# Low halves of the gate weight slabs: from GpSimd's subtraction to an accumulating DMA

## What is computed

```
def conv_glu_ffn(h_norm, w_in, conv_w, conv_b, w_out):
    gate, up = jnp.split(h_norm @ w_in, 2, axis=-1)      # w_in: 1024 x 5632
    padded = jnp.pad(gate, ((0, 0), (CONV_WIDTH - 1, 0), (0, 0)))
    conv = conv_b
    for t in range(CONV_WIDTH):                          # 3 taps over the tokens
        conv = conv + padded[:, t:t + S, :] * conv_w[t]
    return (jax.nn.silu(conv) * up) @ w_out              # w_out: 2816 x 1024
```

## Time and profile before

| | us |
|---|---|
| median of 3 runs | 1417.29 |
| lowest and highest run | 1416.80, 1419.93 |
| span of the profiled execution, first to last instruction | 1418.1 |

### The profile page before, as it was taken

The page is one execution under the profiler, slowest core; times in us unless marked ns, Lnnn a source line. Parts: engine busy times, 40 slices in busy tenths (PEclk is TensorE's granted clock), DMA queues, the critical chain, the costliest instruction groups (busy, mean ns, idle before and its releaser), DMA issues.

```text
span 1418.1 us, 17472 instructions
## 1 busy us (share of the span) xinstructions
PE 1400.8 (99%) x6863; PEld 1149.9 (81%) x6863; DVE 766.2 (54%) x1120; ACT 621.9 (44%) x1080; POOL 666.8 (47%) x371
## 2 busy tenths in 40 slices
PE   8999999999999999999999999999999999999999
PEld 6888778887788888888888887788778888888887
DVE  5574675565776305663165655836657652066611
ACT  6747482755433212333346555735753322132321
POOL 5635654552444444444346367535344444444443
PEclk9999999999999999999999999999999999999999
DMA  6332002331233323333333220223223333333322
GB/s 181 94 97 72 18 23 88 115 106 58 76 117 90 102 91 104 104 89 97 97 90 102 86 60 15 75 68 112 89 67 97 104 89 97 100 97 97 100 91 87
DMA packets 176305, 125.67 MB, mean 89 GB/s; under 512 B 14657, under 2 KB 152672, under 8 KB 176224
## 3 DMA queue, kind: packets, MB, share of 16 engines
q1 hardware_dynamic: 175664, 124.55, 29.5%
q10 hardware_dynamic: 560, 0.01, 0.0%
HBM read 122.44 MB, written 2.10 MB: 88 GB/s over the span
## 4 chain that ended last, share of the span: by engine, by line
PE 95%; DVE 2%; issue 1%; ACT 1%; DMA 1%; SPq 0%; DVEq 0%
PE bank L639 28%; PE bank L643 28%; PE bank L641 28%; PE bank L813 2%; PE bank L942 1%; PE bank L943 1%; PE bank L801 1%; PE bank L1022 1%; PE bank L982 1%; DVE Q L1831 1%; PE bank L1097 1%; DVE scores_h L1863 1%; PE bank L921 1%; DMA x_tok<-in_x 1%; DVE scores_g L1863 1%
## 5 line engine op out<-in xcount | busy, mean ns | idle before, releaser
L565 POOL TENSOR_TENSOR w_lo<-raw,w_hi 128x1024 fp32r<-128x1024 f32 (+2 forms) x230 | 545.9, 2377 | 664.8 <-ACT w_hi L1173 663.2
L1173 ACT ACTIVATE w_hi<-raw 128x1024 fp32r<-128x1024 f32 (+3 forms) x229 | 236.5, 1035 | 331.0 <-PE bank L643 330.6
L639 PE MATMUL bank<-x_hi,w_hi 128*128 128x512 f32 x944 | 371.4, 393 | 3.3 <-issue 1.6
L643 PE MATMUL bank<-x_hi,w_lo 128*128 128x512 f32 x944 | 367.5, 389 | 0.0
L641 PE MATMUL bank<-x_lo,w_hi 128*128 128x512 f32 x944 | 367.4, 389 | 0.0
L639 PEld LDWEIGHTS bank<-x_hi,w_hi 128*128 128x128 f32 x944 | 177.2, 188 | 46.1 <-issue 6.5
L641 PEld LDWEIGHTS bank<-x_lo,w_hi 128*128 128x128 f32 x944 | 177.2, 188 | 37.4 <-issue 1.4
L643 PEld LDWEIGHTS bank<-x_hi,w_lo 128*128 128x128 f32 x944 | 177.2, 188 | 37.3
L1950 DVE SCALAR_TENSOR_TENSOR conv<-gate_in,gains_all,conv 128x512 f32<-128x512 f32 x44 | 118.1, 2685 | 1.6
L1537 ACT ACTIVATE conv_silu<-conv 128x512 f32<-128x512 f32 x44 | 27.8, 632 | 169.5 <-DVE conv L1951 169.5
L1673 DVE TENSOR_TENSOR h<-h,bank 128x512 f32<-128x512 f32 x48 | 31.8, 681 | 105.2 <-PE bank L643 105.1
(11 more groups left out here) (318 smaller groups left out, 2276.2 us busy)
## 6 DMA issues: line engine op xcount, KB each, us to landing
raw<-in_w_ffn_in SPq DMA_DIRECT2D x88, 512.0 KB, 3.8
raw<-in_w_ffn_out SPq DMA_DIRECT2D x40, 512.0 KB, 3.6
raw<-in_w_in SPq DMA_DIRECT2D x27, 512.0 KB, 3.8
raw<-in_w_mix_out SPq DMA_DIRECT2D x16, 512.0 KB, 3.9
raw<-in_w_ca_kv SPq DMA_DIRECT2D x32, 256.0 KB, 3.2
raw<-in_w_ca_q SPq DMA_DIRECT2D x8, 512.0 KB, 3.4
raw<-in_w_ca_out SPq DMA_DIRECT2D x8, 512.0 KB, 3.8
raw<-in_w_in SPq DMA_DIRECT2D x12, 256.0 KB, 2.9
```

The source lines that it names most:

```text
L565: pool.tensor_tensor(w_lo[gi % SPLIT][:, c0:n], raw[gi % RAW][:, c0:n], w_hi[gi % SPLIT][:, c0:n].bitcast(f32), ALU.subtract).then_inc(S[" ...
L639: pe.matmul(o, ah, bh, start=first, stop=False)
L643: mm = pe.matmul(o, al, bh, start=False, stop=last)
L1173: act_.activation(w_hi[k % SPLIT][:, 0:n], raw[k % RAW][:, 0:n], ACT.Copy).then_inc(S["hi_split"], 1)
```

## The change

For the gate slabs alone, the low half is made otherwise. ACT writes `w_lo = -raw`, rounded to fp32r, which is the negated high half, ahead of its copy to `w_hi` (semaphore `negated`). POOL, in place of its subtraction, waits for `negated` and issues a DMA that adds `raw` to `w_lo` (`accum_op=ALU.add`), whose landing counts 16 on `lo_in` of the buffer. PE and SP wait for that semaphore, and for `hi_split` besides. All other slabs keep POOL's subtraction.

```diff
+    FIRST_DMA_LOW = slab_at["gate", 0, 0]
+    slab_names = {i: name for name, i in slab_at.items()}
+    pool_lows, dma_lows = {}, {}
+    for gi in range(DEPTH * NS):
+        if gi % NS >= FIRST_DMA_LOW and slab_names[gi % NS][0] == "gate":
+            dma_lows[gi] = 16 * (sum(j % SPLIT == gi % SPLIT for j in dma_lows) + 1)
+        else:
+            pool_lows[gi] = len(pool_lows) + 1
...
+        def low_ready(gi):
+            return (lo_in[gi % SPLIT], dma_lows[gi]) if gi in dma_lows else (S["lo_split"], pool_lows[gi])
...
                         if gi >= RAW:
-                            sp.wait_ge(S["lo_split"], gi - RAW + 1)
+                            sp.wait_ge(*low_ready(gi - RAW))
+                            if gi - RAW in dma_lows:
+                                sp.wait_ge(S["hi_split"], gi - RAW + 1)
...
+                        if gi in dma_lows:
+                            pool.wait_ge(S["negated"], sum(j <= gi for j in dma_lows))
+                            pool.dma_start(w_lo[gi % SPLIT][:, 0:n], raw[gi % RAW][:, 0:n], accum_op=ALU.add).then_inc(lo_in[gi % SPLIT], 16)
+                            continue
                         pool.wait_ge(S["hi_split"], gi + 1)
...
-                        pe.wait_ge(S["lo_split"], i + 1)
+                        pe.wait_ge(*low_ready(i))
+                        if i in dma_lows:
+                            pe.wait_ge(S["hi_split"], i + 1)
...
                             if k >= SPLIT:
                                 act_.wait_ge(*released[k - SPLIT])
+                            if k in dma_lows:
+                                act_.activation(w_lo[k % SPLIT][:, 0:n], raw[k % RAW][:, 0:n], ACT.Copy, scale=-1.0).then_inc(S["negated"], 1)
                             act_.activation(w_hi[k % SPLIT][:, 0:n], raw[k % RAW][:, 0:n], ACT.Copy).then_inc(S["hi_split"], 1)
```

More of the change, by code:

```diff
@@ L306, in build_trunk @@
         pb = [ctx.enter_context(nc.psum_tensor(f"bank{i}", [P, 512], f32)) for i in range(8)]
-        names = """lo_split hi_split slab_used spread_in mem_in rows_t gains_ready chain_v chain_a chain_p
+        names = """lo_split hi_split negated slab_used spread_in mem_in rows_t gains_ready chain_v chain_a chain_p
             hT_mm h_in h_sq_done h_sq_sum r_cols_mm hk_mm hk_evac x_hi_done x_lo_done r_done r_diag_done r_mm r_bc_done
@@ L320, in build_trunk @@
         raw_in = [ctx.enter_context(nc.semaphore(f"raw_in{i}")) for i in range(RAW)]
+        lo_in = [ctx.enter_context(nc.semaphore(f"lo_in{i}")) for i in range(SPLIT)]
+        def low_ready(gi):
+            return (lo_in[gi % SPLIT], dma_lows[gi]) if gi in dma_lows else (S["lo_split"], pool_lows[gi])
         x_in = [ctx.enter_context(nc.semaphore(f"x_in{t}")) for t in range(NT)]
@@ L391, in build_trunk @@
         PER_LAYER = dict(
-            lo_split=NS, hi_split=NS, spread_in=16 * (1 + len(spread_of)), mem_in=16 * MT, zeroed=7, pair_prod=1, lat_sq_sum=2, tab_done=8,
+            spread_in=16 * (1 + len(spread_of)), mem_in=16 * MT, zeroed=7, pair_prod=1, lat_sq_sum=2, tab_done=8,
             qk_prod=1, scores_base=2 * NT, decays_done=len(BLOCKS), k_level=2 * len(BLOCKS), h_sq_done=3 * KD, h_sq_sum=3, r_cols_mm=2, rope_mm=1, lat_mm=4,
```

## The result

The changed kernel takes 1425.87 us (median of 4 runs, 1423.85 to 1429.09) against 1417.33 us before; the ratio is 1.0063, with an interval of 1.0051 to 1.0075. That is 8.5 us or 0.6% slower. The profiled execution has a span of 1422.1 us, at the fast end of its runs, and only 4.0 us over that of before. That difference of two executions is not the cost: before's execution lost some 4.1 us at 138 to 197 us, where the changed kernel's did not, far from anything the change touches; the changed kernel's lost 1.6 us at 840 us.

The account below looks back on a forecast made before the run. PE was taken to bound the kernel. With D = 5.7, waits of 2.36 and 3.15 us in layer 0, 2.36 and 2.71 in layer 1 made 10.6 us, added to the 1417.29 median: 1427.9 us, range 1419.5 to 1442.3.

Parts of the forecast that it names:

- What bounds the kernel: PE, busy 1400.8 of 1418.1 us at the 2.4 GHz level; only its waits matter, relieving POOL is worth nothing.
- The four tight places: gate(0,1) and gate(0,3) in both layers: 2.55 to 3.34 us until PE's first use; waits there sum to 10.6 us.
- gate(0,4) is covered by the wait at gate(0,3): Layer 0: gate(0,4) has only 4.15 us, but PE's wait at gate(0,3) delays its use and not its split.
- D: Time from the negation's end through POOL's issue, DMA and semaphore until PE may start; taken as 5.7 us.
- POOL and DVE: DVE's taps and POOL's subtractions hold each other up; first tap 0.55 us alone, 2.32 beside gate(0,3)'s subtraction.
- Relief of some 2 to 4 us reaches DVE only from chunk 2 on. Worth nothing on PE's path.: Fewer POOL subtractions free DVE only where gate slabs have enough slack; no gain for PE.
- I cost the negations at nothing: 44 negations of 1.05 us on ACT, 46 us, taken as hidden; uncovered at the four tight places, 4 us.
- PE waits D - S: At a gate slab PE waits D less S, the time from the old split's end to PE's first use.
- Rival A: The DMA lands like a plain load, D under 3.75 us, so it is hidden and the time not slower; chance 0.13.
- Rival B: Slow accumulation, D over 6.85 us: gate(1,0), then every second rhythm slab waits; 1444 us at 8; chance 0.25.
- Rival C: DVE's relief reaches PE through chunks 0 and 1, at most 1.3 us; 0.02 with anything else gaining over 0.2%.

Follow-up runs that it names:

- spare_tight: Changed kernel with gate(0,1) and gate(0,3) of both layers back on GpSimd's subtraction, 40 DMAs kept: 1417.61 us, ratio to before 1.0002.
- up_later: Accumulating DMA for 38 up slabs, all but up(0,0), up(0,1), up(0,3) of each layer, instead of the gate slabs: 1415.81 us, ratio to before 0.9987.
- tight_only: Changed kernel with the DMA only for gate(0,1) and gate(0,3) of both layers, the other 40 gate slabs subtracted: 1429.46 us, ratio to before 1.0081.
- negate_only: Changed kernel without accumulating DMAs: ACT negates all 44 gate slabs, then POOL subtracts over them as before: 1421.29 us, ratio to before 1.0023.
- late_1: Changed kernel with one idle memset on POOL ahead of each accumulating DMA: 1437.13 us, ratio to before 1.0136.
- late_2: Changed kernel with two idle memsets on POOL ahead of each accumulating DMA: 1470.03 us, ratio to before 1.0370.
- after_again: The changed kernel once more, word for word, with its own profile: 1425.61 us, ratio to before 1.0059.
- up_slabs: Accumulating DMA for 42 up slabs, all but up(0,0), instead of the gate slabs: 1417.19 us, ratio to before 0.9997.

## Why the prediction was right, and what was off in it

The forecast was 1427.9 us, +10.6; measured were +8.5, inside the range, by the mechanism that was named. That it came as close as it did is partly luck: a term that was too large and one that was missing made up for each other. By its steps:

- **What bounds the kernel.** Right in the main: forty of the 44 exchanges left the time as it was (spare_tight). POOL's busy time was forecast 106 us lower and is 69 lower, since the issues themselves occupy it for 39; that cost nothing. But the "2.4 GHz level, all along" was read from a row of 35 us slices in tenths, which hides short falls: the mean granted clock of that very execution is 0.995, and at 138 to 146 us it is 0.57.
- **The four tight places.** Right. They are the only slabs that PE waits for in the changed kernel, and taking them back takes the whole measurable cost back. That gate(0,4) is covered by the wait at gate(0,3) was right as well; with that wait at its old 1.3 us, gate(0,4) waits 0.75 us.
- **D.** Taken as 5.7, bounds 2.9 to 7.6; it measured 4.99. The estimate by the bytes read, 5.0, would have hit, but by chance: it had no room for POOL's issue, and the rows show 0.36 us to the issue, 4.54 to the landing, 0.09 to PE. The sum with 4.99 gives 7.7 us of waits; 7.1 came in. D alone was worth 2.8 us of the forecast's 10.6.
- **POOL and DVE.** DVE's side of it holds, in the first tap of chunk 2 and in the second tap of up_later. The rows of before do not show the other side, where the prediction lets the trace agree with "hold each other up": beside the long tap, POOL's subtraction took its usual 2.37 us.
- **"Relief of some 2 to 4 us reaches DVE only from chunk 2 on. Worth nothing on PE's path."** Wrong, on the good side. POOL's missing subtractions also free DVE ahead of chunk 0, in the chains of `x_lo` and of the norm's squares, and gate(0,1)'s negation starts 6.16 us behind PE's first gate matmul, where the split started 6.63 us behind it. tight_only, which lacks that relief, waits 1.72 and 1.65 us there for 1.29 and 1.38.
- **"I cost the negations at nothing."** Right for the sum, by a cover that I had not named. Alone they cost 3.3 us (negate_only), with a wait grown by 0.95 us ahead of gate(0,0) in each layer, where I had reckoned only with the 9 us of the slab itself and not with the bank that DVE frees. The relief of DVE pays for it.
- **"PE waits D - S."** Incomplete. Behind a wait the clock may fall, and matmuls at half speed are added: 1.4 to 2.9 us where it happens. The 1.4 us between the waits' 7.1 and the measured 8.5 are probably this; in tight_only, late_1 and late_2 the rows show it. D was taken too large by 2.8 us in the sum and this term was left out, which is how the forecast came close.
- **Rival A** (hidden) fell: D was over 3.75. The estimate after the Trainium skill's "DMA: Bandwidth & Descriptors", section "Anatomy of one DMA", 3.2 us, is 1.4 us under the 4.6 us measured from issue to landing. That section names no accumulating DMA, and the measurement decides. **Rival B** did not occur, and late_2 shows it as it was described, each second gate slab waiting about 1.0 us where D - 7.65 is 1.2. **Rival C**: DVE's relief did reach PE's path, by under 1 us ahead of gate(0,1) in this kernel, and by 1.4 us in up_later, where it shortens chunk 0.

What stays open: why the clock falls behind a given wait in one execution and not in another. The changed kernel and after_again are the same program with the same waits, and only one shows it behind gate(0,3) of layer 0. Filling the pause was tried in one layer of one kernel only, with one profile.

## What to carry to other kernels

An engine that idles half its time is not the place to save: look for the consumer's slack, slab by slab, and send the longer path only where the slack exceeds it. The same accumulating DMA cost 0.6% at 44 slabs of which four had 2.5 to 3.3 us, nothing measurable at the other 40, and gained 0.1% at slabs with slack whose subtraction had been slowing VectorE. Price a new wait of TensorE at more than its length, because the matmuls behind it may run at half clock, and look for such falls in short stretches, since a page in slices averages them away; and price a DMA with what else is issued in the same microsecond.

## What the runs showed of the hardware

- An accumulating DMA of 512 KB, from SBUF into SBUF, issued by GpSimd: it occupies GpSimd 0.88 us (44 of them, 0.87 to 1.02), landed 4.5 to 4.6 us after the issue in 32 of 44 cases, 8.3 and 8.6 us after it beside two loads of 512 KB issued within 0.5 us (the changed kernel), and 6.8 to 7.5 us after it beside one issued within 0.1 us (up_slabs).
- TensorE's granted clock fell from its 2.4 GHz to its 1.2 GHz level as it stood still for 2.0 to 7.7 us in a dense stretch, or just behind, for up to some 6 us, but not in each execution; behind pauses of 0.8 to 1.96 us no profile shows a fall. With the pause filled by matmuls it stayed up, in the one profile taken.
- A subtraction of GpSimd held VectorE up also in the chain ahead of the FFN: an `x_lo` of 0.75 us took 2.38 us beside it (before and negate_only).
